# Five seams of a four-stage trunk: loads, entries and a group of weight sums rearranged together

## The reference

```python
x = x + gmlp_mixer(rms_norm(x, norm_mix_g[0]), ...)   # gelu(h @ w_in) -> u, v (2048 each)
x = x + swiglu(rms_norm(x, norm_ffn_g[0]), ...)       # d_ff = 2816
x = x + chunk_attention(rms_norm(x, norm_mix_g[1]), ...)  # 16 heads, band of 9 chunks of 64
x = x + swiglu(rms_norm(x, norm_ffn_g[1]), ...)
return rms_norm(x, final_g)
```

## Time and profile before

| | us |
|---|---|
| median of 3 runs | 2608.01 (2607.97 to 2608.17) |
| profiled execution, own time | 2607.87 |
| its span, first to last instruction | 2606.1 |
| PE busy | 2459.5 (94%) |
| DVE / POOL / ACT busy | 1684.9 / 1295.1 / 1002.8 |

### The profile page before, as it was taken

One profiled execution on the slowest core, in us unless ns is written; L12 is line 12 of the kernel. 1 busy time (PEld: TensorE's weight loads), 2 busy tenths in 40 slices (PEclk: granted clock), 3 DMA queues, 4 the chain that ended last, 5 costly groups with the idle time before them and its releaser, 6 DMA issues. The chain is left out here.

```text
span 2606.1 us, 36363 instructions
## 1 busy us (share of the span) xinstructions
PE 2459.5 (94%) x11464; PEld 2024.2 (78%) x11464; DVE 1684.9 (65%) x2669; ACT 1002.8 (38%) x1815; POOL 1295.1 (50%) x908
## 2 busy tenths in 40 slices
PE   8998999999899999998889999999888999999997
PEld 6887888877688888876767777777766888888876
DVE  5246666667576777666756666676675667677756
ACT  4112111224344333331465555566642334433323
POOL 4242223222788787877212012221125877888776
PEclk9998999999999999999999999999999999999998
DMA  4223122111111211111110011111011111111111
...
DMA packets 70522, 143.74 MB, mean 55 GB/s; under 512 B 7312, under 2 KB 17696, under 8 KB 69936
## 3 DMA queue, kind: packets, MB, share of 16 engines
q1 hardware_dynamic: 52912, 119.72, 14.3%
...
...
## 5 line engine op out<-in xcount | busy, mean ns | idle before, releaser
L703 POOL TENSOR_TENSOR a_lo<-raw_block,a_hi 128x512 fp32r<-128x512 f32 x364 | 510.3, 1402 | 152.1 <-ACT a_hi L1554 128.0
L665 POOL TENSOR_SCALAR w_hi<-raw 128x1024 fp32r<-128x1024 f32 x80 | 91.1, 1139 | 847.0 <-PE bank L914 601.0
L1554 ACT ACTIVATE a_hi<-raw_block 128x512 fp32r<-128x512 f32 x312 | 195.9, 629 | 342.5 <-PE bank L914 143.7
L912 PE MATMUL bank<-T_hi,a_hi 128*128 128x512 f32 x672 | 264.0, 393 | 7.8 <-issue 7.1
L914 PE MATMUL bank<-T_hi,a_lo 128*128 128x512 f32 x672 | 263.1, 391 | 0.0
L913 PE MATMUL bank<-T_lo,a_hi 128*128 128x512 f32 x672 | 262.7, 391 | 0.0
L912 PE MATMUL bank<-B_hi,a_hi 128*128 128x512 f32 x576 | 225.2, 391 | 2.6 <-DVE h_full L2004 1.8
L914 PE MATMUL bank<-B_hi,a_lo 128*128 128x512 f32 x576 | 224.2, 389 | 0.0
L913 PE MATMUL bank<-B_lo,a_hi 128*128 128x512 f32 x576 | 224.2, 389 | 0.0
L667 POOL TENSOR_TENSOR w_lo<-raw,w_hi 128x1024 fp32r<-128x1024 f32 x80 | 198.4, 2480 | 6.7
L2004 DVE TENSOR_TENSOR h_full<-bank,h_full 128x512 f32<-128x512 f32 x54 | 37.3, 691 | 212.2 <-PE bank L914 211.8
...
## 6 DMA issues: line engine op xcount, KB each, us to landing
...
```

The lines of the kernel that those rows point to most:

```text
L665: pool.tensor_scalar(w_hi[slot][:, :], raw[r][:, :], 1.0, 1.0, ALU.mult, ALU.mult).then_inc(w_split, 1)
L703: pool.tensor_tensor(out, full, r32(hi), ALU.subtract).then_inc(made, 1)
L912: pe.matmul(out, lh, rh, start=start, stop=False, skip_group_check=read_between)
L1554: act.activation(a_hi[pos][:, :], src[:, :], ACT.Copy).then_inc(w.left_hi, 1)
```

## The change

Five pieces. (1) SP issues weight unit 2 before x's second half and unit 3 in the middle of it. (2) The loads of v's first group and of w_s are issued by ACT at the middle of V's last chunk; after V only the first half's v parts are made before the mixing; the rest of the first norm (tiles 4 to 7 of x's second half) and the second half's v parts follow in G's first event, ACT's part of that between its gelu and its high copy, DVE's ahead of the event; the loads of the next group come behind event 0. (3) The gate group of the feed-forward's second chunk is a middle group: high copies by ACT, and POOL leaves the first chunk at product 10; in the first chunk PE finishes banks 1 and 3 first, DVE's order is rewritten, and ACT takes the second chunk's banks before its high copies. (4) Attention's entry: the squares of x's second half are taken among the last additions; q and k of the first half are projected together and v after them, with the mean at tile 2 and the spread at tile 5; DVE's tiles of the second half are mixed with the low parts; scores 0 to 7 wait only for k's first half, and a one-column Exp is run ahead. (5) In the last norm the squares go to PSUM banks 1 and 3, ACT copies the second rstd to SBUF, and POOL finishes two of the eight tiles of the second half.

SP, the names that tables give, and PE:

```diff
@@ line 89
-MID_MADE = 20 + GROUP
+MID_MADE = 20 + MID
@@ line 101
+AT_G0_SECOND = AT_G1 - 1
@@ line 131
-MADE_SECOND, MADE_LAST = 20, middle(LATE, AT_D_LATE, MID, MID_MADE + MID)
+MADE_FIRST, MADE_LAST = 20, middle(LATE, AT_D_LATE, MID, MID_MADE + MID)
@@ line 369
-def square_buffer(k):
-    return tmp[1 + k % 2]
+def square_buffer(n, h, k):
...
+    return bank[1 + 2 * (k % 2)] if (n, h) == (4, 1) else tmp[1 + k % 2]
...
+POOL_OUT = 2
@@ line 379
-return bank[1 + h] if n == 0 else norm_bank
+return bank[1 + h] if n == 0 else bank[3] if (n, h) == (2, 1) else norm_bank
@@ line 392
-return {(0, 1): bank[0], (1, 0): bank[3]}.get((n, h), norm_bank)
+return {(0, 1): bank[0], (1, 0): bank[3], (2, 1): bank[3]}.get((n, h), norm_bank)
@@ line 462
-order[pair][:3] = [(("k", 0), 0), (("v", 0), 1), (("q first", 1), 2), (("k", 1), 1)]
+order[pair][:3] = [(("k", 0), 0), (("v", 0), 1), (("q first", 1), 0), (("k", 1), 2)]
@@ line 556
-load_x(1, range(KT))
-for u in range(RAW, 3 * RAW):
+unit(RAW, 0, 2)
+load_x(1, range(4))
+unit(RAW + 1, 1, 4)
+load_x(1, range(4, KT))
+for u in range(2 * RAW, 3 * RAW):
@@ line 601
-sp.wait_ge(s.prod, 12)
+sp.wait_ge(s.prod, 10)
@@ line 629
-gate_up(1, 1, lambda op: MADE_SECOND + MADE[op], first_order)
+gate_up(1, 1, lambda op: middle(1, AT_G0_SECOND, MID, MID_MADE + MIDDLE[op]), order)
@@ line 651
-for k in range(KT):
-    sp.wait_ge(y_full, k + 1)
+for k in range(POOL_OUT, KT):
+    sp.wait_ge(y_full, k - POOL_OUT + 1)
...
+    if k % 3 == 1:
+        n = k // 3 - 1
+        sp.wait_ge(y_pool, KT + n + 1)
+        sp.dma_start(out_t[n][:, toks(1)], x[:, n, toks(1)]).then_inc(y_out, 16)
@@ line 1149
-pe.wait_ge(s.made, MADE_SECOND)
+pe.wait_ge(s.made, MADE_FIRST)
@@ line 1158
+        tile(bank[2 * up + 1], 5 + 2 * up, "B22", k, False, k == 3, s.prod if k == 3 else None)
+for up in range(2):
+    for k in range(4):
...
-for k in range(4):
-    for up in range(2):
-        tile(bank[2 * up + 1], 5 + 2 * up, "B22", k, False, k == 3, s.prod if k == 3 else None)
-down(0, "first", 1, 8, ((0, 3), (1, 4)))
+down(0, "first", 1, 8, ((1, 3), (0, 4)))
@@ line 1295
+    pe.wait_ge(p_read, p_number(it, "k", 0) + 1)
+    pe.wait_ge(k2_zero, 2)
+if s == 8:
...
-    pe.wait_ge(k2_zero, 2)
@@ line 1345
-project([fill(-1, "q", 0)[:, :], fill(0, "k", 0)[:, :], fill(0, "v", 0)[:, :]], 0, u, 0, 2,
-        p_done, ((6, lambda: mean(2, 1)),), each=True)
-spread(2, 1)
+project([fill(-1, "q", 0)[:, :], fill(0, "k", 0)[:, :]], 0, u, 0, 2,
+        p_done, ((2, lambda: mean(2, 1)), (5, lambda: spread(2, 1))), each=True)
+project([fill(0, "v", 0)[:, :]], 2, u + 2, 0, 2, p_done)
```

GpSimd and ScalarE:

```diff
@@ line 736
-pool.wait_ge(s.left_hi, middle(it, at, 7, slot + 1))
+pool.wait_ge(s.left_hi, middle(it, at, 7, 7 + slot + 1))
@@ line 839
-pool.wait_ge(s.prod, N_PROD.first)
+pool.wait_ge(s.prod, 10)
...
-group(3, lambda op: MADE_SECOND + MADE[op], lambda op: None)
+middle_group(it, AT_G0_SECOND)
@@ line 902
+pool.wait_ge(sq_done, 8 * (NH2 * 4 + 1) + POOL_OUT)
+pool.sem_inc(taken, 1)
+for k in range(POOL_OUT):
+    pool.tensor_scalar(x[:, k, toks(1)], x[:, k, toks(1)], gain[:, 4, k:k + 1], None, ALU.mult
+                       ).then_inc(y_gained, 1)
+pool.wait_ge(rstd_copied, 4)
+for k in range(POOL_OUT):
+    pool.wait_ge(y_gained, KT + k + 1)
+    pool.tensor_tensor(x[:, k, toks(1)], x[:, k, toks(1)], rstd[1][:, :], ALU.mult).then_inc(y_pool, 1)
@@ line 1455
+for store in v_out:
+    act.wait_ge(store, 2 * 16)
+act.wait_ge(rel_out, 16)
+for h in range(NH2):
+    load_v(0, h)
+load_ws(0)
@@ line 1496
-if not last:
+def load_next():
...
+if not first and not last:
+    load_next()
...
-def event(j):
+def gelu(j):
...
+def event(j, between=lambda: None):
+    gelu(j)
+    between()
...
-    if f == 1 and not last:
+    if j % 2 == 1 and not last:
...
-for j in range(3):
-    event(j)
+def rest_of_norm():
+    hi_tiles(0, 1, 4)
+    v_his(0, 1)
...
+if first:
+    for store in v_out:
+        act.wait_ge(store, 2 * CB * 16)
+event(0, rest_of_norm if first else lambda: None)
+if first:
+    load_next()
+event(1)
+event(2)
@@ line 1577
-for k in range(2):
+for k in range(4):
...
+silu(held[:, 1, :], hidden_part(h_full, 1, 1))
+hi(0, 3, 1, 1)
+act.wait_ge(w.prod, 10)
+for pos in range(2):
+    left_high(1, AT_G0_SECOND, pos)
+act.wait_ge(w.cadd, 3)
...
-hi(0, 3, 0, 1)
-act.wait_ge(w.cadd, 3)
-silu(held[:, 1, :], hidden_part(h_full, 1, 1))
-hi(0, 4, 1, 1)
-for k in range(2, 4):
-    right_hi("T2", k, full_lo["T2"], 20 + 3 * k + 1)
-    right_hi("T4", k, full_lo["T4"], 20 + 3 * k + 3)
+hi(0, 4, 0, 1)
+for pos in range(2, 4):
+    left_high(1, AT_G0_SECOND, pos)
+act.wait_ge(w.prod, 12)
+for pos in range(4, 7):
+    left_high(1, AT_G0_SECOND, pos)
@@ line 1625
-hi_tiles(n + 1, 0)
-squares(n + 1, 1)
-std(n + 1, 1)
+if n == 3:
+    squares(4, 1)
+    std(4, 1)
+    copy_rstd(4, 1)
+    return
+for k in range(3):
+    if k < 2:
+        hi_tiles(2, 0, k, k + 1)
+    square(2, 1, k)
+for k in range(3, KT):
+    square(2, 1, k)
+    if k > 5:
+        hi_tiles(2, 0, k - 4, k - 3)
+hi_tiles(2, 0, 4, 6)
+std(2, 1)
+hi_tiles(2, 0, 6, KT)
@@ line 1664
-behind_gate(0)
...
+    behind_gate(0)
...
-behind_gate(1)
+    behind_gate(1)
...
+if kind == "second":
+    behind_gate(0)
+    behind_gate(1)
...
-behind_gate(2)
+    behind_gate(2)
...
+if kind == "second":
+    behind_gate(2)
@@ line 1756
+hi_tiles(2, 1, 0, 2)
...
-hi_tiles(2, 1)
+hi_tiles(2, 1, 2, KT)
+act.activation(warm[:, :], eps[:, :], ACT.Exp)
@@ line 1817
-for r in range(4):
-    act.wait_ge(v_out[r], 2 * CB * 16)
-act.wait_ge(rel_out, 16)
-for h in range(NH2):
-    load_v(0, h)
-load_ws(0)
-hi_tiles(0, 1, 4)
...
-for h in range(NH2):
-    v_his(0, h)
+v_his(0, 0)
```

VectorE:

```diff
@@ line 1959
+if first:
+    dve.wait_ge(v_done, CB * BLOCKS)
+    tiles(0, 1, range(4, KT))
+    v_los(0, 1, range(4))
@@ line 2088
-for k in range(5):
-    if k < 4:
-        scaled(k, k, full_lo["T3"][:, k, :])
-        scaled(k, 4 + k, b22_full[:, k, :])
-    if k:
-        right_lo("T1", k - 1, full_lo["T2"], 8 + 2 * k)
-    if k < 4:
-        difference(full_lo["T2"], full_lo["T3"], full_lo["T2"], k, 8 + 3 * k + 1)
-    if k:
-        right_lo("B22", k - 1, b22_full, 8 + 2 * k)
-    if k < 4:
-        add(0, "first", 0, 0, 2 * k)
-        add(0, "first", 0, 0, 2 * k + 1)
-t2_t3_t4(0)
-t2_t3_t4(1)
+def t3(k):
+    scaled(k, k, full_lo["T3"][:, k, :])
...
+def b22(k):
+    scaled(k, 4 + k, b22_full[:, k, :])
...
+def t1(k):
+    difference(full_lo["T2"], full_lo["T3"], full_lo["T2"], k, 8 + 3 * k + 1)
...
+def t1_lo(k):
+    right_lo("T1", k, full_lo["T2"], 8 + 2 * (k + 1))
...
+def b22_lo(k):
+    right_lo("B22", k, b22_full, 8 + 2 * (k + 1))
...
+t3(0)
+b22(0)
+t1(0)
+add(0, "first", 0, 0, 0)
+add(0, "first", 0, 0, 1)
+t1_lo(0)
+add(0, "first", 0, 0, 2)
+b22_lo(0)
+add(0, "first", 0, 0, 3)
+t3(1)
+b22(1)
+add(0, "first", 0, 0, 4)
+t1(1)
+add(0, "first", 0, 0, 5)
+t3(2)
+t1_lo(1)
+add(0, "first", 0, 0, 6)
+b22_lo(1)
+add(0, "first", 0, 0, 7)
+b22(2)
+t1(2)
+t3(3)
+t1_lo(2)
+b22_lo(2)
+b22(3)
+t1(3)
+t1_lo(3)
+b22_lo(3)
+for k in range(4):
+    t2_t3_t4(k)
...
-cadd(held[:, 0, :], bank[0])
+cadd(held[:, 1, :], bank[1])
...
-cadd(held[:, 2, :], bank[2])
+cadd(held[:, 3, :], bank[3])
...
-times(held[:, 2, :], 0, 1)
+times(held[:, 3, :], 1, 1)
+t2_t4_lo(2)
...
-cadd(held[:, 1, :], bank[1])
-lo(0, 3, 0, 1)
+cadd(held[:, 0, :], bank[0])
+lo(0, 3, 1, 1)
...
-cadd(held[:, 3, :], bank[3])
+cadd(held[:, 2, :], bank[2])
...
-times(held[:, 3, :], 1, 1)
-t2_t3_t4(2)
-lo(0, 4, 1, 1)
-add(0, "first", 1, 8, 0)
-add(0, "first", 1, 8, 1)
-t2_t3_t4(3)
-add(0, "first", 1, 8, 2)
-add(0, "first", 1, 8, 3)
-t2_t4_lo(2)
-add(0, "first", 1, 8, 4)
-add(0, "first", 1, 8, 5)
-t2_t4_lo(3)
-add(0, "first", 1, 8, 6)
-add(0, "first", 1, 8, 7)
+times(held[:, 2, :], 0, 1)
+right_lo("T2", 3, full_lo["T2"], 16 + 2 * 3 + 2)
+lo(0, 4, 0, 1)
...
+    add(0, "first", 1, 8, k)
+right_lo("T4", 3, full_lo["T4"], 16 + 2 * 3 + 2)
+for k in range(4, KT):
+    add(0, "first", 1, 8, k)
+right_lo("T3", 0, full_lo["T3"], 24 + 1)
+dve.wait_ge(w.prod, N_PROD.at(1, PROD["A12"]))
+dve.wait_ge(w.snap, N_SNAP.at(1, 1))
+cadd(gated[0][:, :], bank[1])
+for k in range(1, 4):
@@ line 2180
-    for k in range(KT):
+    dve.wait_ge(rstd_copied, 4)
+    for k in range(POOL_OUT, KT):
...
-ops = tile_ops(2, 0)
-for k in range(KT):
-    ops[k]()
+tile_full(2, 0, 0)
+add(it, "last", 1, 8, 0)
+tile_full(2, 0, 1)
+add(it, "last", 1, 8, 1)
+tile_lo(2, 0, 0)
+add(it, "last", 1, 8, 2)
+add_squares(2, 1, 1)
+add(it, "last", 1, 8, 3)
+tile_lo(2, 0, 1)
+for k in range(4, KT):
...
-for op in ops[KT:]:
-    op()
-sum_squares(2, 1)
+    add_squares(2, 1, k - 2)
+tile_full(2, 0, 2)
+add_squares(2, 1, 6)
+tile_full(2, 0, 3)
+tile_lo(2, 0, 2)
+add_squares(2, 1, 7)
+for k in range(4, 7):
+    tile_full(2, 0, k)
+    tile_lo(2, 0, k - 1)
...
+tile_full(2, 0, 7)
+tile_lo(2, 0, 6)
+tile_lo(2, 0, 7)
@@ line 2220
-product(0, "A12")
-snap(1)
-cadd(gated[0][:, :], bank[1])
...
+    product(0, "A12")
+    snap(1)
```

(43 more changed lines are left out.)

4 lines of the change are left out of this document (2 added, 2 removed).

## The result

| | before | changed |
|---|---|---|
| median, us (lowest to highest) | 2608.09 (2607.97 to 2610.88), 4 runs | 2569.42 (2569.19 to 2570.11), 4 runs |
| profiled execution, own time / span | 2607.87 / 2606.1 | 2570.11 / 2568.0 |

What follows compares the result with a forecast made beforehand. PE was busy 94% of the span, so only seams between stages, each a stand plus slow matmuls, could give time. 3.8 + 0.5 + 15.0 + 15.2 + 1.3 = 35.8 off 2607.87 gave 2572; range 2558 to 2586.

Steps and rivals of the forecast that it cites:

- PE waits 2.73 us at 24.64: V's start: PE's wait for weight unit 2's low part goes, 2.73 us, and 1.6 us of slow matmuls with it.
- waits for the second gelu: V's entry: the projection at 217.84 waits for the second gelu, which gets new work ahead; it starts 0.9 us earlier.
- the end of -8: V's entry: the far end of the term's range, where all of PE's stand before the mixing would go, 8 us.
- two items, 2.9 and 4.4: Each feed-forward: 2.9 us from earlier hidden parts and additions, 4.4 from the stand at 690.70 with its slow stretch.
- slow clock as before: Feed-forward, behind the waits for the hidden parts: slow-clock matmuls stay as they were, so no gain was counted.
- 2.3 of slow matmuls: Attention's entry: 2.3 us of slow-clock matmuls counted as gained, within the term of 15.2 us.
- that now read two SBUF operands: The end: six last DVE multiplies read two SBUF operands beside POOL's two, so they take 6.0 us, not 5.36.
- D: Feed-forward's middle chunks: the stand of 690.70 comes back, 4.2 us each; 2631 with every second one; chance 0.03.
- E: All seams: what PE saves at each is waited for at the next; within 0.2%, 2607 us; chance 0.03.
- B: More holding by POOL: hidden parts stay late, each feed-forward gives 2.9 us instead of 7.5; 2581 us; chance 0.13.
- C: Attention's entry falls to its poor end, softmax late; 2578 us; chance 0.09.
- A: Less holding: DVE slips past POOL at start, feed-forwards (6 us more each) and end; about 2558 us; chance 0.10.

Runs made afterwards that it cites:

- e1: The changed kernel with V's loads put back in their old order; 2571.33 us, 0.9861 of the kernel before.
- e8: The changed kernel run once more with no edit, as the yardstick for the runs beside it; 2569.64 us, 0.9842 of the kernel before.
- e7: The changed kernel with ACT's second gelu of V's first gated group directly behind its first; 2573.67 us, 0.9858 of the kernel before.
- e4: The changed kernel with attention's entry put back as before; 2585.22 us, 0.9909 of the kernel before.
- e6: The changed kernel with POOL and the loads' queue waiting for product 12, not 10, at the end of feed-forward's first chunk; 2566.16 us, 0.9827 of the kernel before.

## Why the prediction was right, point by point

The total was forecast at 2572 and came at 2569.4. The seams and their mechanisms were right; the sizes were less good than their sum. In the table parts 1, 2 and 4 gained 2.6 us less than forecast and parts 3 and 5 5.3 us more; that half of this cancels is luck. Some 9 of the 38.7 us go with a higher clock, and how much of that the slow matmuls counted in the terms cover is open.

- **Part 1, 3.8: mis-sized.** The step that failed took "PE waits 2.73 us at 24.64" and its slow stretch as the old order's price. The wait went, as forecast, but with the same old order e1 waits 0.47. The charge of 0.5 for DVE's operations held by POOL was right in kind: e8 waits 0.64 for one. The part is worth 0.4 to 0.7 at its seam and 1.4 at equal clock. That the two traces agreed with the forecast (3.5) was chance, since both used the same profiled execution of before.
- **Part 2, 0.5: right in kind.** Mixing at 202, a stand behind it, the projection held by the second gelu and, 3.15 us gained before it, forecast at 213.75 and seen at 213.57; -0.4 to 0.9. The step "waits for the second gelu" named the last of the waits and not the product of event 0 that came 1.6 us ahead of it. Had I made the end of -8 a claim ("all of the stand"), e7 would have shown it wrong: three edges had to go, not one.
- **Part 3, 7.5 each: right in kind, the second too small.** Its two items, 2.9 and 4.4, add up to 7.3. Shifted by the 3.15 us gained before it, the parts were forecast at 651.65 and 657.35; PE had them at 651.41 and 656.49. The waits in front of them were forecast at some 3 us and are 0.95 and 2.05, because PE itself came 2.0 later than forecast, 1.7 of it by a slow stretch at 581. The gains are 8.6 and 11.1 (against e8 7.1 and 10.5). The step that failed is "slow clock as before". Before had slow stretches of 6.8 and 3.4 us in both feed-forwards (at 661 and 692, and at 1982 and 2013); in the first profile of the changed kernel there is one of 3.4 us behind the waits of the first, and none behind those of the second. The price of a contended pair, taken from rows, holds: 652.98 to 654.68 is 1.70 us. By the rule of the Trainium skill that the prediction cites (SBUF — State Buffer, "SBUF: two separate sides") it would be 1.90, 0.60 and 1.30 one after the other; the trace is on the rows' side. The total can't decide it, since the 2.6 us between the two are less than what other terms missed.
- **Part 4, 15.2: somewhat too large, within its ends.** Its steps stand: 1.5 us lost at tile 2 (1.5), 30.8 us to the scores (31). Behind the scores 1.9 us are lost, not 1.4 (the query is read at 1293.4), with a short slow stretch. The two traces have 13.75 (14.0 against e8), e4 11.4 to 12.9 at the seam. Before's matmuls behind its two stands were slow for 6.8 and 10.2 us; the term counted "2.3 of slow matmuls" as the part's own, and at one clock e4 is 9.4 from the changed kernel.
- **Part 5, 1.3: right sum, one wrong step.** The multiplies "that now read two SBUF operands": they read the spread in PSUM, as before, and six take 4.04 us beside POOL's two, unheld, where I had 6.0. The gain is 1.9 to 3.0. The held additions were sized right (1.18 to 0.68). The mean still takes 1.87 in the first profile, where full clock was expected; in e8 it takes 1.05:

```profile
2556.64 1.05 PE L967 MATMUL probs_t<-ones,tmp 128*128 128x1 f32 x8 [2.17 <-DVE tmp L1901]
```

- **Rivals.** D and E fell: no wait over 0.5 us in PE's middle chunks between 700 and 1112. B fell (8.6 and 11.1 where it had 2.9), C fell (part 4 kept 13.75 of its 15.2). A's mechanism holds at the end alone, and e6 shows what it was worth in the feed-forward: 4.4 us each, 3.8 net, which the change had given away by letting POOL go at product 10.
